# Decay differences of the gated recurrences: from GpSimd to VectorE, and the next job's first two levels made ahead

## The reference, cut to what matters

```
cum    = cumsum(log_g)                                  # per key channel
scores = sum_d q[i,d] * k[j,d] * exp(cum[i,d] - cum[j,d])    for i >= j
o      = scores @ v  +  (q * exp(cum)) @ state
state  = exp(cum[last]) * state  +  (k * exp(cum[last] - cum))^T @ v
o      = rms_norm(o) * silu(gate)
```

## Time and profile before

| | us |
|---|---|
| median of 3 runs (3131.3 to 3134.19) | 3133.27 |
| the profiled execution's own time | 3131.03 |
| its span | 3129.2 |
| TensorE busy | 3033.6 (97%) |
| VectorE busy | 1245.5 (40%) |
| GpSimd busy | 1043.4 (33%) |
| ScalarE busy | 917.1 (29%) |

### The profile page before, as it was taken

The page is one execution under the profiler, slowest core; times in us unless marked ns, Lnnn a source line. Parts: engine busy times, 40 slices in busy tenths (PEclk is TensorE's granted clock), DMA queues, the critical chain, the costliest instruction groups (busy, mean ns, idle before and its releaser), DMA issues.

```text
span 3129.2 us, 35710 instructions
## 1 busy us (share of the span) xinstructions
PE 3033.6 (97%) x14710; PEld 2493.5 (80%) x14710; DVE 1245.5 (40%) x2353; ACT 917.1 (29%) x1341; POOL 1043.4 (33%) x513
## 2 busy tenths in 40 slices
PE   8999999999999999999999999999999999999998
PEld 7777788888888877777777777788888788888886
DVE  8848532212122164554436543532545211111115
ACT  3224242121211234333424443432323212111111
POOL 4344363232322352111422332232223633333335
PEclk9999999999999999999999999999999999999999
DMA  6341211121111122111110111124330212111111
GB/s 207 83 140 58 88 54 48 48 68 47 48 48 47 54 76 68 56 53 54 41 48 28 54 54 48 41 68 168 128 135 28 64 44 68 48 48 49 52 41 54
DMA packets 70897, 207.62 MB, mean 66 GB/s; under 512 B 11376, under 2 KB 19968, under 8 KB 70720
## 3 DMA queue, kind: packets, MB, share of 16 engines
q1 hardware_dynamic: 70736, 205.34, 20.5%
HBM read 172.54 MB, written 32.77 MB: 66 GB/s over the span
## 4 chain that ended last, share of the span: by engine, by line
PE 86%; DVE 4%; POOL 3%; ACT 3%; issue 3%; DMA 0%; SPq 0%; ACTq 0%; DVEq 0%; POOLq 0%
PE PS L436 48%; PE PS L476 7%; PE PS L478 7%; PE PS L477 7%; PE PS L755 3%; PE PS L1066 3%; POOL WL L2539 2%; PE PS L943 1%; PE PS L973 1%; PE PS L502 1%; PE PS L858 1%; PE PS L857 1%; PE PS L856 1%; PE PS L563 1%; PE PS L956 1%
## 5 line engine op out<-in xcount | busy, mean ns | idle before, releaser
L2539 POOL TENSOR_TENSOR WL<-WR,WH 128x1024 fp32r<-128x1024 f32 x241 | 580.7, 2417 | 1853.3 <-ACT WH L1166 1853.2
L436 PE MATMUL PS<-XH,WH 128*128 128x512 f32 x2176 | 691.4, 399 | 16.8 <-DVE XL L1789 9.1
L436 PE MATMUL PS<-XL,WH 128*128 128x512 f32 x2176 | 674.6, 391 | 0.0
L436 PE MATMUL PS<-XH,WL 128*128 128x512 f32 x2176 | 672.5, 390 | 0.0
L436 PEld LDWEIGHTS PS<-XH,WH 128*128 128x128 f32 x2176 | 397.3, 189 | 108.4 <-issue 25.3
L436 PEld LDWEIGHTS PS<-XL,WH 128*128 128x128 f32 x2176 | 410.5, 189 | 87.6
L436 PEld LDWEIGHTS PS<-XH,WL 128*128 128x128 f32 x2176 | 409.8, 188 | 87.8
L1166 ACT ACTIVATE WH<-WR 128x1024 fp32r<-128x1024 f32 x241 | 253.2, 1055 | 665.3 <-PE PS L478 443.3
L476 PE MATMUL PS<-WH,HH 128*128 128x512 f32 x736 | 286.4, 389 | 2.5 <-POOL HL L2571 2.5
L478 PE MATMUL PS<-WH,HL 128*128 128x512 f32 x736 | 286.3, 389 | 0.0
L477 PE MATMUL PS<-WL,HH 128*128 128x512 f32 x736 | 286.3, 389 | 0.0
(11 more groups left out here) (349 smaller groups left out, 3971.2 us busy)
## 6 DMA issues: line engine op xcount, KB each, us to landing
WR<-in_weights SPq DMA_DIRECT2D x241, 512.0 KB, 3.6
gates<-EG SPq DMA_DIRECT2D x18, 512.0 KB, 5.2
EI<-gates SPq DMA_DIRECT2D x18, 512.0 KB, 4.8
BR<-brbuf SPq DMA_DIRECT2D x12, 512.0 KB, 6.2
RAWX<-in_xT SPq DMA_DIRECT2D x8, 512.0 KB, 7.2
spill<-STQ SPq DMA_DIRECT2D x16, 256.0 KB, 2.3
RX<-in_x SPq DMA_DIRECT2D x8, 512.0 KB, 6.2
xbuf<-XF SPq DMA_DIRECT2D x8, 512.0 KB, 2.6
```

Of the source, the lines that this page charges most:

```text
L436: last = e.matmul(PS[:, u.b + h, :], w, x[:, k, 512 * h:512 * h + 512], start=k == 0 and w is w1 and x is xh, stop=k == nk - 1 and w is w2)
L2539: e.tensor_tensor(WL[:, v % NSPL, :], WR[:, v % NRAW, :], WH[:, v % NSPL, :].bitcast(F), ALU.subtract).then_inc(w_lo, 1)
```

## The change

- `level_diff` and the difference for the state's keys move from GpSimd to VectorE. The state's difference is written into `KX` itself, no more into DD0, and ScalarE takes exp in place.
- VectorE's `begin(j + 1)` (differences of levels 0 and 1 and of the state's keys) stands in job j, after its outputs and ahead of its norm. ScalarE's `begin(j + 1)` and `begin_rest(j + 1)` (the exps of levels 0 and 1, KX, the last columns, QXX) stand after job j's outputs, ahead of the rest of the fill.
- In iteration n VectorE does: scaled operands of level n, `keep` of level n - 1, difference of level n + 2.
- The scaled operands of level 0 of job j + 1 are made on VectorE once the last `cy` transposes of job j are full, ahead of job j's two staging products.
- GpSimd keeps the two memsets and the `WL` cuts.
- `YG` moves from the place of DD0/DD1 to that of `KQ`.

```
-        YG = sb("YG", 116, [128, 8, 256])
+        YG = sb("YG", 124, [128, 8, 256])
# ScalarE
             def begin(j):
                 level_exp(j, 0)
+                level_exp(j, 1)
+            def begin_rest(j):
+                CU, base = INP[j % 2][2], 128 * (j % 2)
+                e.wait_ge(c_dx, j + 1)
+                e.activation(KX[:, :], KX[:, :], ACT.Exp, scale=-1.0).then_inc(c_a, 1)
                 if j:
                     e.wait_ge(c_o, 8 * j)
                 e.wait_ge(c_cum, j + 1)
...
-                if j:
-                    begin(j)
-                    begin_rest(j)
                 fill.tick(per[0])
...
+                if j < 5:
+                    begin(j + 1)
+                    begin_rest(j + 1)
                 fill.rest()
# VectorE
+            def level_diff(j, n):
+                if n >= 2 or j:
+                    e.wait_ge(c_kq, 7 * j + max(n - 1, 0))
+                e.tensor_tensor(dv, cv_, cv_[:, :, s - 1:s].to_broadcast([128, 512 // s, 2 * s]), ALU.subtract).then_inc(c_d, 1)
+            def begin(j):
+                e.wait_ge(c_cum, j + 1)
+                level_diff(j, 0)
+                level_diff(j, 1)
+                if j:
+                    e.wait_ge(c_o, 8 * j)
+                e.tensor_tensor(KX ..., cu3, cu3[:, :, 127:128].to_broadcast([128, 8, 128]), ALU.subtract).then_inc(c_dx, 1)
+            def scaled(j, n):        # the two products of before, and their waits
+                if n == 0:
+                    for key in (("cq", j), ("ck", j)):
+                        e.wait_ge(lots[key].drained, lots[key].ndrained)
...
+                    if 0 < n < 7 or n == 0 and j == 0:
+                        scaled(j, n)
                     if n:
                         keep(j, n - 1)
+                    if n + 2 < 7:
+                        level_diff(j, n + 2)
...
                     fill.tick(per[2])
+                if j < 5:
+                    begin(j + 1)
...                                   # norm, YG, fill.rest()
+                if j < 5:
+                    u = lots["cy", j, nh - 1]
+                    e.wait_ge(u.full, u.nfull)
+                    scaled(j + 1, 0)
...                                   # staging products L2477
+            e.wait_ge(lots["dy", 3].full, lots["dy", 3].nfull)
+            begin(0)
# GpSimd: level_diff, its calls and the difference for the state's keys are gone
```

More of the change, by code:

```diff
@@ L2402, in scan @@
                 t.then_inc(c_cum, 1) if i == 7 else t.then_inc(dve, cv.up())
+            def level_diff(j, n):
+                s = LEVELS[n]
+                cv_ = INP[j % 2][2][:, :].rearrange("p (n c) -> p n c", c=2 * s)
+                dv = DDs[(n + 1) % 2][:, :].rearrange("p (n c) -> p n c", c=2 * s)
+                if n >= 2 or j:
[5 more added lines that the diff above has]
+                level_diff(j, 1)
+                cu3 = INP[j % 2][2][:, :].rearrange("p (i c) -> p i c", i=8)
+                if j:
+                    e.wait_ge(c_o, 8 * j)
+                e.tensor_tensor(KX[:, :].rearrange("p (i c) -> p i c", i=8), cu3, cu3[:, :, 127:128].to_broadcast([128, 8, 128]),
+                                ALU.subtract).then_inc(c_dx, 1)
+            def scaled(j, n):
+                Q_, K_ = INP[j % 2][0:2]
+                s = LEVELS[n]
+                v4 = lambda x: x.rearrange("p (n c) -> p n c", c=2 * s)
+                kb, D_ = KQ[:, n % 2, :], DDs[(n + 1) % 2]
+                if n == 0:
+                    for key in (("cq", j), ("ck", j)):
+                        e.wait_ge(lots[key].drained, lots[key].ndrained)
+                if n >= 2:
+                    for hh in range(gated_job(j)[0]):
+                        e.wait_ge(lots["lv", j, n - 2, 1, hh].full, lots["lv", j, n - 2, 1, hh].nfull)
+                e.wait_ge(c_e, 7 * j + n + 1)
+                e.tensor_tensor(v4(kb)[:, :, 0:s], v4(K_[:, :])[:, :, 0:s], v4(D_[:, :])[:, :, 0:s],
+                                ALU.mult).then_inc(dve, cv.up())
+                e.tensor_tensor(v4(kb)[:, :, s:2 * s], v4(Q_[:, :])[:, :, s:2 * s], v4(D_[:, :])[:, :, s:2 * s],
+                                ALU.mult).then_inc(c_kq, 1)
             def compute(j, fill, per):
@@ L2409, in compute @@
                 fill.tick(per[0])
-                for key in (("cq", j), ("ck", j)):
-                    e.wait_ge(lots[key].drained, lots[key].ndrained)
                 for n in range(8):
@@ L2702, in pool_gated @@
         def pool_gated(e):
[L2703 to L2711, removed]
             finish(cuts(pool_cut, e, "glr"))
             def begin(j):
-                nh, CU = gated_job(j)[0], INP[j % 2][2]
+                nh = gated_job(j)[0]
                 s = lots["cy", j - 1, gated_job(j - 1)[0] - 1] if j else lots["dy", 3]
                 e.wait_ge(s.full, s.nfull)
[L2718 to L2722, removed]
                 e.memset(ST[:, 0:nh, :], 0.0).then_inc(c_st, 1)
                 e.memset(SG_[:, :, :], 0.0).then_inc(c_sg, 1)
-                level_diff(j, 1)
             finish(chain(cuts_keys(pool_cut, e, 0), cuts(pool_cut, e, ("cq", 0))))
@@ L2735, in pool_gated @@
                                  cuts_early(pool_cut, e, BESIDE_JOB[j]))
-                per = JOB_TICKS[j]
                 if j:
                     begin(j)
[L2739 to L2743, removed]
                 finish(fill)
```

## The result

| | median us | runs |
|---|---|---|
| before | 3133.11 | 4 (3131.3 to 3134.19) |
| changed | 3110.45 | 4 (3107.61 to 3112.35) |

Ratio 0.9923, 95% interval [0.9911, 0.9935]: faster by 0.8%, by 22.7 us between the medians. The forecast was 3115 with a range of 3110 to 3126. The direction and the mechanism were right, the gain was put too small: 17.9 us.

What follows compares the result with a forecast made beforehand. TensorE, busy 3033.6 of 3129.2 us, was taken as the bound, so only its waits and clock count. Terms 6.57 + 4.93 + 4.23 + 3.4 - 1.2 = 17.9 us off 3131.03 give 3113.1, by the runs 3115; range 3110 to 3126.

Steps and rivals of the forecast that it cites:

- waits at level 0, jobs 2 to 5: TensorE's four waits for scaled operands at the start of these jobs would go, gaining 6.57 us.
- slow clock behind them, jobs 3 to 5: Matmuls after three waits of about 1.85 us at level 0 would run at full clock, gaining 4.93 us.
- waits at level 2, jobs 2 to 4: TensorE's three waits of 1.41 us for scaled operands would go, gaining 4.23 us.
- job 1, levels 0 to 7: Level 4's wait for `keep` to free banks would shrink by 1.8 us, plus 1.6 of slow clock: 3.4 us gained.
- `STG`'s store, job 2: Level 1 would wait for the later staging store: 1.2 us lost, with ends of 0 and 2.4 + 1.6.
- Part 1: At job boundaries, the next job's beginning made ahead removes level 0's waits, 6.57 us, and their slow clock, 4.93 us.
- job 0's end: The tightest place for ScalarE's added work: 5.9 of 7.11 us of free time used, so VX isn't delayed.
- Part 2: Differences of levels 2 to 6 on VectorE remove level 2's waits, 4.23 us, and job 1's at level 4, 3.4.
- margin of 0.4 us: At level 2, operands would be ready at 1761.1 us, before TensorE comes at 1761.6.
- Inner waits stay: Rival, chance 0.19: only the boundary is mended, level 2 and job 1's level 4 stay late; gain 11.5, runs 3122 us.
- VectorE becomes the bound: Rival, chance 0.08: in the levels VectorE needs 8.6 us against TensorE's 7.33, making the kernel slower, runs 3156 us.
- The gain is eaten by new waits: Rival, chance 0.09: waits for `STG`'s store, VX in job 0 and banks eat about 11 of 17.9 us; runs 3128.

Runs made afterwards that it cites:

- levels on GpSimd: The changed kernel with the differences of levels 2 to 6 back on GpSimd, the next job's beginning still ahead on VectorE: 3122.07 us, ratio 0.9962.
- all on GpSimd: The changed kernel's order with every difference made on GpSimd, the next job's beginning after the outputs' ticks: 3120.23 us, ratio 0.996.
- each difference twice: The changed kernel with each difference of levels 2 to 6 made twice on VectorE, 30 more ops: 3120.95 us, ratio 0.9949.

## Why the prediction was right, and where it was too small

Each term against the distances between the same products in both profiles:

| step | forecast | measured |
|---|---|---|
| waits at level 0, jobs 2 to 5 | 6.57 | 1.18 + 2.04 + 2.03 + 2.03 = 7.28 |
| slow clock behind them, jobs 3 to 5 | 4.93 | 1.72 + 1.75 + 1.73 = 5.20 |
| waits at level 2, jobs 2 to 4 | 4.23 | 1.57 + 1.56 + 1.57 = 4.70 |
| job 1, levels 0 to 7 | 3.4 | 53.92 - 49.94 = 3.98 |
| `STG`'s store, job 2 | -1.2 | 0 |
| clock fall near 1724 us | none | 1.63 |
| levels 2 to 7 of jobs 2 to 4, small steps | none | 1.12 |
| clock fall in job 3's outputs | none | -1.49 |

The measured ones make 22.4 together, of 22.6 (the rest are steps under 0.1). The last row is luck of one execution: without it, as in the second profile of the changed kernel, the stage gave 24.1. By its runs that repeat was 0.9934 of the kernel before, 3112.4 of 3133.1, so the lower end of the range was missed narrowly.

**Part 1 was right in mechanism.** The four waits went (and one hold that had been allowed for did come: a cut held the second of job 2's two products for 2.89 us, without harm), the norm behind three more ops was hidden, and job 0's end held: ScalarE stood idle 1.61 us ahead of VX where I had 1.2. At level 4 of job 1 I had expected a wait of under 1 us to be left; there was none, but one of 0.74 at level 5, and job 1 gave 3.98 us and not 3.4.

**Taking a removed wait at its row was too small, by 0.17 us each.** The rows 6.57 and 4.23 of the sum are off by this. All seven waits for KQ gave 0.16 to 0.19 us more than the idle time of TensorE's matmul side. The weight side's waits show where it is: in the same stretch of the kernel before it reads

```profile
PEld PS L1066 <- issue: 22.7, 25, 2.9
```

against 6.3 in 15 now. While TensorE waits, the next weights aren't loaded; when nothing is waited for, they load beneath the last matmul. That this is the whole of the 0.17 is only argued, not shown by an experiment.

**The steps that failed are two terms of the sum: the store, put at -1.2 us, and the clock near 1724 us, put at nothing.** For a late `STG` I took a loss of 1.2 us in job 2; it was 0. VectorE after the change, in job 2, and the landing of the two `STG` stores:

```profile
1738.01 1.27 DVE L2511 SCALAR_TENSOR_TENSOR STG<-PS,cols,GS 128x1024 f32<-128x1024 f32 x1
1739.20 1.21 DVE L2411 TENSOR_TENSOR DD<-LG 128x1024 f32<-128x1024 f32 x1
1744.35 0.69 DVE L2437 TENSOR_TENSOR KQ<-KT,DD 128x512 f32<-128x512 f32 x1 [3.94 <-DMA brbuf<-STG]
...
DMA to landing us min/median/max: 2.8/3.9/5.0
```

VectorE did wait 3.94 us for it, but the operands were there at 1745.6 and TensorE came at 1747.24. To compare with the prediction, which counted in the times of the kernel before, add 5.96 us (TensorE wanted level 1 at 1753.2 there). `STG` was then finished at 1745.2, at the late end of the forecast 1742.2 to 1745.4, as a cut did come between. The store took 5.0 us and not 5.6 to 6.7, so it landed at 1750.3, within the forecast 1748.5 to 1752.1, and the margin was 1.6 us, within "from 3 us to nothing". So the picture was right, and the -1.2 was the wrong price for it: nearly all of its own margin said no loss, and the shorter landing kept it so.

**TensorE's clock was counted by one profile's places.** I charged a fall to the waits of 1.85 and 2.48 and none to that of 1.42 near 1724 us, which had one: the granted clock from 1724.5 to 1728.5 us was 0.57 there, and 1.00 behind the same wait after the change. It mostly went with another: in four of the five profiles with a fall at job 1's level 4 near 1672 (before, twice; levels on GpSimd; all on GpSimd) it was there. In the fifth (each difference twice) it wasn't, and neither in the five others that have this wait, though it is the same in all. Why it went is not shown. Together the store and this fall are 2.8 of the 4.6 us that the stage gave beyond the forecast; the waits' 0.17 each, job 1 and the short steps, less the fall in job 3's outputs, make up the rest. The range left these out: the best ends that I gave for the store and for job 1 bring the sum to 20.0 us, and no term stood for a fall at another place.

**Part 2 held, and so did the rule of the lock.** The differences' times after the change (ns min/median/max), and those of the products:

```profile
L2411 DVE TENSOR_TENSOR DD<-LG x42: 1191/1211/3430, 1502.7 to 2044.9; 128x1024 f32<-128x1024 f32 x42
L2437 DVE TENSOR_TENSOR KQ<-KT,DD x42: 665/684/2902, 1508.3 to 2052.1; 128x512 f32<-128x512 f32 x42
```

A median of 1.21, as taken from L2431, and 3.43 where a cut holds one. Job 2's level 2 went as drawn up, one op held by the cut and the second free (VectorE, then GpSimd's cut):

```profile
1750.62 2.90 DVE L2437 TENSOR_TENSOR KQ<-KT,DD 128x512 f32<-128x512 f32 x1
1753.44 0.68 DVE L2439 TENSOR_TENSOR KQ<-QT,DD 128x512 f32<-128x512 f32 x1
...
1750.38 2.58 POOL L2575 TENSOR_TENSOR WL<-WR,WH 128x1024 fp32r<-128x1024 f32 x1 [12.69 <-ACT WH L1166]
```

By the Trainium skill, page "SBUF — State Buffer", section "Who interferes with whom", the later of the two is blocked whole; by the rows, 2.90 us for an op of 0.68 that began 0.24 us behind a cut of 2.58. The margin of 0.4 us that worried me came out at 0.4: operands at 1754.1, TensorE at 1754.48.

**The rivals.** "Inner waits stay" is what the variant with the levels on GpSimd does, and it costs 11.4 to 12.9 us against the changed kernel, so this was the right thing to fear for the wrong reason: VectorE had the room. "VectorE becomes the bound" needed more than a second difference in every level. "The gain is eaten by new waits" had one small piece of truth, 0.74 us for `keep` at level 5 of job 1, where the prediction had named such a wait as a sign of being wrong.

## What to carry to other kernels

When one queue serves two users (here GpSimd's cuts and the next job's first step), ask what stands behind what at the boundary: moving the first step up in the order removed that wait on either engine, while inside the levels the other engine did it (another order on GpSimd was not tried there). Where two engines lock each other out, moving work off one also frees the other's ops: the 48 differences take VectorE 65.4 us, but its busy time rose by only 47.5, since its level products alone fell from 94.8 to 77.5 us, and waits went away. After such a change read the list of waits again: what is left there was worth another 10 us, by letting a producer's latency fall behind one slice of other work.

## What the runs showed of the hardware

- The same wait of TensorE need not have the same effect on its clock. In the profiles here, 13 of 15 waits of 1.8 to 2.6 us at a level were followed by half clock (1.2 GHz of 2.4) for a few microseconds, at 1.4 to 1.75 us each; none of 19 waits of 1.4 to 1.6 at a level was. But that of 1.42 us near 1724 us, which comes one set of transposes after an idle time of 0.3 us, was in 4 of 10 profiles, and one of 0.87 behind one of 1.18 in 3 of 30 places.
- One wait shows it best, since it lies behind the stage and is in every profile: TensorE waits 2.48 to 2.51 us between 2445 and 2475 us. It was followed by a fall in 7 of the 12 profiles (granted clock 0.57 to 0.63 in the next 4 us) and by full clock in 5. What decides stays open.
- These falls make up most of the difference between executions of one kernel: waits repeat to 0.03 us, while the stage starts 5.2 us apart in the two profiles of the changed kernel, and 2.2 us in those of the kernel before.
- TensorE's idle row understates what a wait costs by some 0.17 us, besides the clock.
